# Where the adaLN modulation sums, their row batches and the first expert loads stand around an attention layer

## The reference, cut to what matters

```python
ml = silu(c) @ mod_w[i] + mod_b[i]              # 6 * 1024 values: sh1, sc1, g1, sh2, sc2, g2
hl = xl * (1 + sc1) + sh1
# layer 0: differential attention, rotary on the latent q and k, latent queries over latent + context keys
# layer 1: multi-scale pooling mixer
xl = layer_norm(ALPHA * xl + (1 + g1) * yl, ln_g[i, 0], ln_b[i, 0])
tokens = xl * (1 + sc2) + sh2
y2 = moe_ffn(tokens, router, wg, wu, wd)        # 16 experts, 2 per token, each D x D_EXPERT, three matrices
xl = layer_norm(ALPHA * xl + (1 + g2) * y2, ln_g[i, 1], ln_b[i, 1])
```

## Time and profile before

| | us |
|---|---|
| median of 3 runs | 1204.79 (1202.83 to 1206.7) |
| the profiled execution | 1203.59 |
| its span, first to last instruction | 1201.6 |
| PE busy | 1134.2 (94%) |
| DVE busy | 362.4 (30%) |
| ACT busy | 166.6 (14%) |

### The profile page before, as it was taken

How to read it: one execution, slowest core, us unless ns; L and a number is a source line. 1 busy time by engine, 2 the same in 40 slices (tenths; PEclk the granted TensorE clock), 3 DMA queues, 4 the chain that set the end, 5 groups by cost and what they waited for, 6 DMA issues and landing times.

```text
span 1201.6 us, 12396 instructions
## 1 busy us (share of the span) xinstructions
PE 1134.2 (94%) x5288; PEld 494.0 (41%) x5288; DVE 362.4 (30%) x732; ACT 166.6 (14%) x397; POOL 8.0 (1%) x10
## 2 busy tenths in 40 slices
PE   8997998898999999999999889999999999988986
PEld 3553554545444333343333227543333433333322
DVE  1559999673111121111111115212111111111113
ACT  1101233614100000001000005200000100000000
POOL 0000000000000000000000010000000000000000
PEclk9998999899999999999999999999999999999998
DMA  9999896983999999999999999999999999999994
GB/s 397 403 361 368 301 361 261 402 323 155 431 430 430 431 429 429 432 430 431 431 430 430 430 427 427 424 431 430 431 430 430 431 430 431 431 428 432 430 429 181
DMA packets 40441, 480.17 MB, mean 400 GB/s; under 512 B 5056, under 2 KB 6336, under 8 KB 8384
## 3 DMA queue, kind: packets, MB, share of 16 engines
q1 hardware_dynamic: 39328, 476.91, 94.6%
q10 hardware_dynamic: 1056, 2.43, 0.7%
HBM read 476.18 MB, written 1.05 MB: 397 GB/s over the span
## 4 chain that ended last, share of the span: by engine, by line
PE 69%; DMA 23%; DVE 6%; ACT 1%; issue 1%; another core or an unknown queue 0%; DVEq 0%; SPq 0%; ACTq 0%
PE ps L913 41%; DMA ring<-in_moe_wu 12%; DMA ring<-in_moe_wg 8%; PE ps L905 4%; PE ps L921 4%; DMA ring<-in_mod_w 3%; PE ps L662 3%; PE ps L762 2%; PE ps L665 2%; DVE ring L1350 1%; PE ps L725 1%; PE ps L668 1%; PE ps L743 1%; DVE modp L1350 1%; PE ps L578 1%; PE ps L931 1%
## 5 line engine op out<-in xcount | busy, mean ns | idle before, releaser
L913 PE MATMUL ps<-ring,tra 128*64 128x512 f32 x2048 | 454.1, 597 | 24.2 <-DMA ring<-in_moe_wu 19.2
L913 PEld LDWEIGHTS ps<-ring,tra 128*64 128x64 f32 x2048 | 147.5, 138 | 322.6 <-issue 280.8
L913 PE MATMUL ps<-ring,work 128*64 128x512 f32 x1024 | 226.8, 595 | 1.9 <-DVE work L1701 1.9
L913 PEld LDWEIGHTS ps<-ring,work 128*64 128x64 f32 x1024 | 71.6, 137 | 135.6 <-issue 133.3
L1240 ACT ACTIVATE work<-ps 128x512 f32<-128x512 f32 x32 | 19.1, 598 | 506.7 <-PE ps L913 506.7
L1699 DVE TENSOR_TENSOR work<-work,ps 128x512 f32<-128x512 f32 x32 | 22.0, 688 | 206.0 <-PE ps L913 206.0
L1233 ACT ACTIVATE tra<-ps,cols 128x128 f32<-128x128 f32 x128 | 48.2, 457 | 255.1 <-PE ps L905 255.1
L1696 DVE TENSOR_TENSOR work<-ps,work 128x512 f32<-128x512 f32 x32 | 22.1, 692 | 202.3 <-ACT work L1240 202.3
L905 PEld LDWEIGHTS ps<-extra,xn 128*128 128x128 f32 x512 | 61.0, 195 | 24.3 <-issue 22.7
L905 PE MATMUL ps<-extra,xn 128*128 128x128 f32 x512 | 66.9, 285 | 1.4 <-DVE extra L1609 1.4
L921 PE MATMUL ps<-work,extra 64*128 64x512 f32 x256 | 63.6, 615 | 1.6 <-DVE work L1705 1.6
(11 more groups left out here) (191 smaller groups left out, 730.2 us busy)
## 6 DMA issues: line engine op xcount, KB each, us to landing
ring<-in_moe_wg SPq DMA_DIRECT2D x64, 2048.0 KB, 29.8
ring<-in_moe_wu SPq DMA_DIRECT2D x63, 2048.0 KB, 29.8
ring<-in_moe_wd SPq DMA_DIRECT2D x63, 2048.0 KB, 30.0
ring<-in_mod_w SPq DMA_DIRECT2D x40, 1024.0 KB, 9.6
ring<-in_mod_w SPq DMA_DIRECT2D x4, 2048.0 KB, 18.2
ring<-in_attn_wqkv SPq DMA_DIRECT2D x4, 2048.0 KB, 11.3
ring<-in_attn_wo SPq DMA_DIRECT2D x2, 2048.0 KB, 10.9
ring<-in_tokens SPq DMA_DIRECT2D x2, 1024.0 KB, 16.1
```

The lines of the kernel that those rows point to most:

```text
L913: last = mm(ps[SLOTS * h:SLOTS * h + SLOTS, b, :], lhs(k0 + k), w[:, k, h * NB:(h + 1) * NB], start=(k0 + k == 0), stop=(k0 + k == KT - 1) ...
```

## The change

The sums ahead of the steps are six in place of eight, both first ropes stand ahead of the sixth (sum 5), and the steps take sums 6 to 15. Of the four sums left, 16 stands ahead of `job_out(3)`, 17 and 18 behind `norm_heads(1)`, and 19 between the token tiles of the attention's norm, where `rows_sum(1)` was; that goes into `route(0)`, behind the copies of the turned tokens. Row batches 1 to 3 stand at steps 3, 7 and 11 in place of 0, 5 and 9, and batch 4 behind the last projection in place of ahead of the third. Bank 0 takes the last transposes of layer 0, since bank 7 still holds the rows; the second gather, which writes bank 7, waits for `rows_sum(1)`. Expert units 1 to 6 are loaded among the last sums' weights, slots 1 and 3 change places in `FREE`, and `("wo", 1)` and `x` go out ahead of the load of sum 16.

```diff
--- before.py
+++ after.py
@@ -46,7 +46,7 @@
 SH1, SC1, G1, SH2, SC2, G2 = range(6)
 
 RING = 11
-FREE = (10, 4, 8, 5, 9, 6, 7, 2, 3, 1, 0)
+FREE = (10, 4, 8, 5, 9, 6, 7, 2, 1, 3, 0)
 UNIT = 4096
 EU = 6
 BAND = P + 8
@@ -85,14 +85,15 @@
 FILL = {s: [] for s in range(NS + 3)}
 for _s in range(10):
     FILL[_s].append(("g", 10 + _s))
-BATCH_AT = {6: 0, 10: 1, 15: 2, 19: 3}
-
-EARLY_SUMS = 8
+BATCH_AT = {6: 0, 13: 1, 17: 2, 21: 3}
+
+EARLY_SUMS = 6
 STEP_SUMS = 10
+ROPES_AT = 5
 
 LOADS = [("q", 0), 0, 1, ("v", 0), 2, "rows", 3, 4, ("k", 1), 5, 6, 7, 8, ("q", 1), 9, "ahead", 10, 11, 12, ("v", 1), 13, 14,
-         ("wo", 0), 15, 16, 17, ("wo", 1), "x", 18, 19]
-AHEAD = 1
+         ("wo", 0), 15, ("wo", 1), "x", 16, 17, ("e", 1), ("e", 2), ("e", 3), ("e", 4), ("e", 5), 18, ("e", 6), 19]
+AHEAD, ISSUED = 1, 7
 
 
 JOBS = ("cols_0", "rpart_0", "gt_0", "g1_0", "g1_1", "cols_2", "cols_1", "joint_0", "joint_1", "rpart_1", "gt_1",
@@ -482,10 +483,10 @@
                     sp.wait_ge(sem("pv_done"), NS)
                 elif v == 6:
                     sp.wait_ge(sem("oT_done"), 2 * TT)
-                elif v in (7, 8):
-                    sp.wait_ge(sem("half_summed"), 2 * (NSUM - 8 + v))
-                elif v < RING:
-                    sp.wait_ge(sem("unit_used"), NA - RING + v + 1)
+                elif v in (7, 9):
+                    sp.wait_ge(sem("half_summed"), 2 * (NSUM - 1 if v == 7 else NSUM))
+                elif v in (8, 10):
+                    early_used(sp, ("wo", (v - 8) // 2))
                 else:
                     used(sp, v - RING)
 
@@ -503,8 +504,9 @@
                     load(to, of, sem(f"ring_loaded_{s}"))
 
             def load_expert(layer, e):
-                for n in range(AHEAD if layer == e == 0 else 0, EU):
-                    load_unit(layer, e, n)
+                for n in range(EU):
+                    if first_unit(layer, e) + n >= ISSUED:
+                        load_unit(layer, e, n)
 
             for what in LOADS:
                 if what == "rows":
@@ -514,6 +516,8 @@
                         load_unit(0, 0, n)
                 elif what == "x":
                     load(xn[:, :].rearrange("p (t n) -> p t n", t=TT), x[0].rearrange("(t p) n -> p t n", p=P), sem("x_loaded"))
+                elif isinstance(what, tuple) and what[0] == "e":
+                    load_unit(0, what[1] // EU, what[1] % EU)
                 elif isinstance(what, tuple):
                     load_early(what)
                 else:
@@ -837,19 +841,18 @@
             turn_heads(1)
             project(0, 1)
             job(4)
-            row_batch(4)
-            NT_BANK = (4, 6, 5, 7)
+            NT_BANK = ((4, 6, 5, 0), (4, 6, 5, 7))
 
             def turn_normed(layer, t):
 
                 for b in range(2):
                     normed(pe, 2 * layer, t, b)
-                    turn_blocks(NT_BANK[2 * t + b], xn[:, t * D + b * NB:t * D + (b + 1) * NB]).then_inc(sem("nT_done"), 1)
+                    turn_blocks(NT_BANK[layer][2 * t + b], xn[:, t * D + b * NB:t * D + (b + 1) * NB]).then_inc(sem("nT_done"), 1)
 
             project(1, 0)
             turn_normed(0, 0)
             project(1, 1)
-            pe.wait_ge(sem("rows_ready"), 2)
+            row_batch(4)
 
             def open_sums(t, k, start):
 
@@ -862,9 +865,9 @@
 
                 if layer:
                     turn_normed(layer, 0)
-                keep_clock(NT_BANK[2], 3)
+                keep_clock(5, 3)
                 turn_normed(layer, 1)
-                keep_clock(0, 1)
+                keep_clock(1, 1)
                 pe.wait_ge(sem("nT_act"), 2 * (layer + 1))
                 pe.wait_ge(sem("nT_dve"), 2 * (layer + 1))
                 pe.wait_ge(sem("rw_ready"), layer + 1)
@@ -1087,6 +1090,8 @@
                 gather(6, 0).then_inc(sem("gather_done"), 1)
                 pe.wait_ge(sem("ssc_ready"), NE * layer + 1)
                 turn_weights().then_inc(sem("sw_turned"), 1)
+                if layer == 0:
+                    pe.wait_ge(sem("rows_ready"), 2)
                 gather(7, 1).then_inc(sem("gather_done"), 1)
                 for e in range(NE):
                     expert(layer, e)
@@ -1391,10 +1396,10 @@
                 v_.tensor_tensor(to, to, swapped[kind], ALU.add).then_inc(sem("roped"), 1)
 
             for n in range(EARLY_SUMS):
-                if n == 6:
-                    rope_batch(0)
+                if n == ROPES_AT:
+                    for batch in range(2):
+                        rope_batch(batch)
                 unit_sum(n)
-            rope_batch(1)
 
             def heads_variance(t):
 
@@ -1497,11 +1502,12 @@
                     heads_variance(0)
                 if s == NS:
                     norm_heads(0)
+            unit_sum(NSUM - 4)
             job_out(3)
             heads_variance(1)
             norm_heads(1)
-            for n in range(EARLY_SUMS + STEP_SUMS, NSUM):
-                unit_sum(n)
+            unit_sum(NSUM - 3)
+            unit_sum(NSUM - 2)
             job_out(4)
 
             def deviation(n, t):
@@ -1531,7 +1537,7 @@
             def normed_out(layer, t):
 
                 dve.wait_ge(sem("nT_done"), 4 * layer + 2 * t + 2)
-                v_.tensor_copy(nT[:, 4:8, t * P:t * P + P], bank((6, 7)[t]).rearrange("p (k t) -> p k t", k=4))\
+                v_.tensor_copy(nT[:, 4:8, t * P:t * P + P], bank((6, 0 if layer == 0 else 7)[t]).rearrange("p (k t) -> p k t", k=4))\
                     .then_inc(sem("nT_dve"), 1)
 
             def attention_norm():
@@ -1550,7 +1556,7 @@
                     spread(0, t)
                     deviation(0, t)
                     if t == 0:
-                        rows_sum(1)
+                        unit_sum(NSUM - 1)
                 norm(0, zbuf[1][:, NB:D])
 
             def sums_norm(n, ready):
@@ -1621,6 +1627,8 @@
 
                 for t in range(TT):
                     normed_out(layer, t)
+                if layer == 0:
+                    rows_sum(1)
                 dve.wait_ge(sem("logits_done"), layer + 1)
                 dve.wait_ge(sem("router_loaded"), 32)
                 g8 = [P, TT * NG, EG, EG]
```

## The result

The changed kernel takes 1207.15 us (median of 12 runs, 1205.62 to 1208.52), the kernel before 1203.77 us (12 runs, 1202.5 to 1206.7). The ratio is 1.0027, 95% interval 1.002 to 1.0035: slower by 3.4 us. The forecast was 1206.1 us against 1204.79 for the kernel before, that is +1.3 us, in a range from 1200.5 to 1210.0. The direction, the range and the place of the wait came true; the size was 2 us short. The profiled execution has a span of 1204.9 us, 3.3 more than before.

What follows compares the result with a forecast made beforehand. The first expert's start, set by a chain over TensorE and VectorE, bounds the kernel. +2.0 -0.7 +0.1 +1.0 -0.2 -0.9 = +1.3 us on 1203.59, 1204.9; the median 1.2 above gives 1206.1, range 1200.5 to 1210.0.

Steps and rivals of the forecast that it cites:

- The bound: Up to 290 us: the end is the first expert's start, 288.38 us, plus an unaltered stretch; shifts pass one for one.
- Early sums and ropes: Ahead of the steps: no wait counted for ropes, scores 0 open at 104.67, the steps start 9.3 to 9.4 us earlier.
- The moved wait: Group 16 waits 10.7 us for ("v", 1), then 2.0 us of low clock; the steps' last sum ends 2.0 later.
- Steps 10 to 15: VectorE paces; TensorE's clock may stay up, saving the wait for scores 12: -0.7, from -1.5 to +1.1.
- The four late sums: Behind the attention: sum 16 +0.1; sum 18, its load queued behind unit 5, ends later, +1.0, from 0 to 2.
- The price of the moved batch: Row batch leaves the place ahead of the projection at 253.11; ScalarE's norm would still hold the transposes: -0.2.
- The clock behind the last projection: The batch fills the 2.0 us idle ahead of 272.65, so the low clock behind may go: -0.9, -1.5 at most.
- (a): Rival: ("v", 1) lands after 9.4 us or less, group 16 starts at 159.0, 3.1 us earlier: 1203.0; chance 0.22.
- (b): Rival: group 16 does not wait, the steps end 3.8 us earlier, clock stays up: -6.0, 1198.8; chance 0.08.
- (c): Unit 5 and halves behind land 2 us late, sum 18 3 us: 1211.7, or 1209.7 with steps as forecast; chance 0.12.
- (d): Rival: TensorE's clock stays low over transposes, around 268 to 275 us and in the steps: +0.9 +1.8, 1208.8; chance 0.13.

## Why the prediction was right

Each point by the steps of the prediction; shifts are places in the profile after less the same place before.

**The bound.** Right. The first expert came 3.26 us later, the span 3.3 and the median 3.4; the ring was full ahead of it in both. The three experiments on the load of ("v", 1) moved the end of the steps by -12.4, +12.3 and +12.0 us and the time by -12.1, +12.0 and +12.1.

**Early sums and ropes.** Right. No rope waited; VectorE was free at 95.5 and idle for 10.88 us. VectorE began on scores 0 8.9 us earlier, forecast 9.3; the half microsecond that is missing was missing already at group 10, which started at 98.17 against 97.64.

**The moved wait.** Right, and shown by three runs. Forecast: out at 149.6, landed after 12.5 us, group 16 at 162.1, 10.7 us of idle time, 2.0 us of low clock. Measured: 150.36, 13.0, 163.41, 11.01 and 1.8. The steps' last sum came 3.2 us later, where I had said 2.0: the weight went out 0.8 us later than forecast, 0.5 of which was there at group 10, and took 0.5 longer to land. The Trainium skill, DMA: Bandwidth & Descriptors, Anatomy of one DMA, gave an estimate of 6.8 us for 2 MB. Its fit is for transfers that GpSimd issues, and SyncE issued this one; the measured 13.0 us does not agree with it, and neither do the 10.0 us of the same weight in the kernel before with the weight earlier, where nothing had gone out on SP for 17 us ahead of it. In the changed kernel with the weight earlier, out at 131.44, it took 16.9 and landed almost four microseconds ahead of its need.

**Steps 10 to 15.** -0.7 forecast, -0.9 measured (the end of the last attention weights at 231.5 against 229.2, +2.3). The number is right by luck: -0.7 was half of what I gave to a clock that stays up, with +1.1 if it falls. It fell: behind the stand of 2.10 us ahead of the batch, batch and scores 11 took 1.84 and 2.00 us. But it was up again for scores 12, so VectorE waited 0.17 us there, against 1.47. The term for a fall was wrong, not only the choice between the two.

**The step that I left out.** From there to the first projection I had 0.1 us; it was +1.5 (240.33 against 236.56 is +3.8). The gaps of 1.16 and 1.76 us ahead of the last transposes are the same as before, but the lower clock lasted through 232 to 238 us, where before it lasted about 3 us. I had no term for it. The kernel with fillers shows that the stretch can be had at full clock. Nothing shows that the change lengthens it: from the values of step 13 to the first projection TensorE took 6.5 us before, 8.0 in the changed kernel, 6.7 with the weight earlier, 7.9 with both loads moved, and in the kernel before with the later weight, which has no part of the change, 7.9. Each is one profiled execution; why they differ stays open.

**The four late sums.** The load of sum 18 was late by 1.76 us (forecast 0 to 2); with it ahead of unit 5 the kernel was 1.5 us faster by the times and 0.8 by the profile, and the forecast term was 1.0. The price of the moved batch (-0.2) was about right, but its reason was incomplete: the third projection waits, before any wait for ScalarE's norm, for the copy of gate 1 out of PSUM (`job_out` five, L759 of the kernel before). In the profile after, that copy runs from 256.82 to 257.5 and TensorE idles 1.65 us for it. In the run with the batch alone the way from the second projection to the third was 8.73 us, before 8.82.

**The clock behind the last projection.** Forecast -0.9, in the profiled execution -1.4, but the mechanism that I gave, closing the gap with the batch, is not borne out. From the start of the fourth projection to the first expert TensorE takes one of two lengths: 26.0 us in the changed kernel, in the three with one or both loads moved, in the one with fillers at the end, and in the kernel before with the later weight, which has no part of the change. It takes 27.4 us before, and 27.6 in the kernel before with the earlier weight, with the late batch alone, with the late sums in one block and with fillers in both places; the last three have the moved batch. In the kernels without fillers the 26.0 goes with the long stretch ahead of the first projection (7.9 or 8.0 us) and the 27.4 or 27.6 with the short one (6.5 to 6.7). The changed kernel with the weight earlier is the exception, 6.7 and 26.0, and its third projection ran slowly. So I read the +1.5 there and the -1.4 here as one stretch of low clock in one place or in another, and not as effects of the change; each kernel has one profiled execution, and no run isolates what picks the place.

**The sum as measured.** +3.2 (steps) -0.9 (steps 10 to 15) +1.5 (to the first projection) +0.9 (late sums and batch, to the fourth projection) -1.4 (to the first expert) = +3.3, against +2.0 -0.7 +0.1 +0.8 -0.9 = +1.3. Of the 2 us that were missing, 1.2 are in the wait for the weight and 1.4 in the stretch that I left out; the others gave back 0.6. That +1.5 and -1.4 nearly cancel owes nothing to the prediction.

**Rivals.** (a) did not happen: with swap copies beside it the load took 13.0 us. (b) I had called an error of mine on which sum is meant; that it is excluded by the order of loads was right, but its price was wrong. Without the wait the steps end 9.2 us earlier than before, not 3.8, and the kernel gets 8.9 us faster, not 6.0. The prediction gives the ten steps 98 us there (105.8 to 204); its own rates, 8.4 us a step and 3.6 for each of two ropes, give 91, and 92.3 were measured (106.19 to 198.50). What the other 7 us were meant for it does not say. (c) is half true: its first mechanism, the late load of sum 18, was there at the size of the forecast; sum 19 did not run past the last projection (done at 268.6, projection at 272.7). Its second time, 1209.7, does not follow from its terms: +6.9 less the 1.0 on the steps is +5.9, 1210.7. (d) did not show at 277 to 281 us, where the granted clock was 1.00 over the last transposes of the changed kernel; the Trainium skill, TensorE: Matmul & The Clock Gate, Part 4: PE-mode transpose, is neither borne out nor refuted by that, since fillers and router products stand beside them. The long low stretch at 232 to 238 us is transposes and value products by turns, but before the change the clock rose within 3 us over the same work, so it does not settle (d) either.

## What to carry to other kernels

In a queue that waits in order, an entry has two deadlines: it may not stand ahead of what its own wait would block, nor behind an entry whose wait has moved. When work is renumbered or shifted by steps, every other entry in that queue has to be placed again against the event that frees its buffer; here one entry left at its number turned a gain of 8.9 us into a loss of 3.4. Where a lead is wiped out in a single wait, price the kernel without that wait before judging the idea.

## What was not expected of the hardware

A stand of TensorE costs more than its length: behind 11.0 and 9.8 us of idle time, 16 products took 8.81 and 9.14 us in place of 7.03, with a granted clock of 0.50 at 164 to 165 us in the first case. In two profiled executions with the same idle time of 2.02 us ahead of the last transposes, the next products ran once at the lower clock (1.94 us, before) and once at the full one (1.07, the kernel before with the later weight): a gap seen once with a low clock behind it is no proof that closing it gains anything. Where it was closed, with the late batch alone, the clock fell later on and the time did not change. A 2 MB load issued by SP took from 7.9 to 21.1 us to land in the changed kernel alone (issues at 201.5 and 64.8 us), and the second value weight from 10.0 to 18.6 us over the kernels, by the place of its issue in the queue; I put that down to what was issued around it, which no run isolates.
